# Buffers of a fused transformer kernel placed in another order, and the low parts of its routing stage issued later

## What is computed

```python
def reference(...):
    x = first_block(...)    # attention + MLP(4096), then pooling mixer + MLP(4096), final norm
    return second_block(x, ...)

def second_block(x, mem, ...):
    h = x
    # ssd branch, latent attention, merged through w_o, cross attention to mem (256 rows)
    h = h + hierarchical_moe(rms_norm_2(h, norm_moe), w_rg, b_rg, w_re, b_re, w_gate, w_up, w_down)
    return rms_norm_2(h, norm_final)

def hierarchical_moe(h, ...):   # 4 groups x 8 experts = 32, width 256, two per token
    g_sel = argmax(t @ w_rg + b_rg)                 # group
    top_v, top_i = top_k(e_logits[g_sel], 2)        # two experts in it
    act = silu(t @ w_gate[e]) * (t @ w_up[e]) * combine[:, e]
    y = sum_e act @ w_down[e]
```

## Time and profile before

| | us |
|---|---|
| median of three runs | 1258.95 |
| the profiled execution | 1256.77 |
| its span (first to last instruction) | 1254.9 |
| mean granted clock of TensorE | 0.992 |

### The profile page before, as it was taken

One profiled execution on the slowest core, in us unless ns is written; L12 is line 12 of the kernel. 1 busy time (PEld: TensorE's weight loads), 2 busy tenths in 40 slices (PEclk: granted clock), 3 DMA queues, 4 the chain that ended last, 5 costly groups with the idle time before them and its releaser, 6 DMA issues. The chain is left out here.

```text
span 1254.9 us, 22421 instructions
## 1 busy us (share of the span) xinstructions
PE 1205.3 (96%) x9064; PEld 1025.1 (82%) x9064; DVE 783.8 (62%) x1316; ACT 608.1 (48%) x992; POOL 99.1 (8%) x102
## 2 busy tenths in 40 slices
PE   9999999999999999999999999999999999999982
PEld 7989999999999999899999988999999833333320
DVE  6876655556755555999899889869645552222113
ACT  6665544454544454767655586665454321111101
POOL 0000100000100000000000030010100004431301
PEclk9999999999999999999999999999999999999997
DMA  9653655554455565455544384355544989999993
GB/s 305 192 182 122 202 172 195 174 196 135 156 181 182 186 200 161 134 168 168 164 140 135 87 258 167 103 202 168 172 165 130 413 326 404 411 404 406 405 406 139
DMA packets 161045, 270.28 MB, mean 215 GB/s; under 512 B 17625, under 2 KB 126142, under 8 KB 156862
## 3 DMA queue, kind: packets, MB, share of 16 engines
q1 hardware_dynamic: 149872, 260.53, 59.9%
q0 software_dynamic: 10720, 8.42, 2.4%
q10 hardware_dynamic: 366, 0.12, 0.0%
HBM read 287.89 MB, written 13.63 MB: 240 GB/s over the span
## 5 line engine op out<-in xcount | busy, mean ns | idle before, releaser
L2118 DVE TENSOR_TENSOR weights_parts<-ring,weights_parts 128x1024 fp32r<-128x1024 f32 (+3 forms) x312 | 363.5, 1186 | 149.2 <-ACT weights_parts L1541 148.8
L1541 ACT ACTIVATE weights_parts<-ring 128x1024 fp32r<-128x1024 f32 (+3 forms) x312 | 308.6, 1009 | 157.2 <-PE psum L885 156.6
L883 PE MATMUL psum<-xnorm_parts,weights_parts 128*128 128x256 f32 x852 | 245.4, 288 | 4.9 <-DVE xnorm_parts L2266 2.0
L884 PE MATMUL psum<-xnorm_parts,weights_parts 128*128 128x256 f32 x852 | 239.4, 281 | 0.0
L885 PE MATMUL psum<-xnorm_parts,weights_parts 128*128 128x256 f32 x852 | 239.2, 281 | 0.0
L883 PE MATMUL psum<-expert_cols,weights_parts 128*128 128x256 f32 (+1 forms) x688 | 194.7, 283 | 3.2 <-DVE expert_cols L2136 2.0
L885 PE MATMUL psum<-expert_cols,weights_parts 128*128 128x256 f32 (+1 forms) x688 | 192.0, 279 | 0.0
L884 PE MATMUL psum<-expert_cols,weights_parts 128*128 128x256 f32 (+1 forms) x688 | 192.0, 279 | 0.0
L883 PE MATMUL psum<-hidden_parts,weights_parts 128*128 128x256 f32 x640 | 181.9, 284 | 2.7 <-DVE hidden_parts L2589 1.7
L884 PE MATMUL psum<-hidden_parts,weights_parts 128*128 128x256 f32 x640 | 180.5, 282 | 0.0
L885 PE MATMUL psum<-hidden_parts,weights_parts 128*128 128x256 f32 x640 | 180.4, 282 | 0.0
(11 more groups left out here) (449 smaller groups left out, 1725.8 us busy)
## 6 DMA issues: line engine op xcount, KB each, us to landing
ring<-in_mlp_w_up SPq DMA_DIRECT2D x32, 1024.0 KB, 5.5
ring<-in_mlp_w_down SPq DMA_DIRECT2D x32, 1024.0 KB, 4.9
ring<-in_w_in SPq DMA_DIRECT2D x30, 1024.0 KB, 5.4
ring<-in_attn_w_qkv SPq DMA_DIRECT2D x12, 1024.0 KB, 6.8
expert_raw<-in_w_exp_gate SPq DMA_DIRECT2D x22, 512.0 KB, 11.4
expert_raw<-in_w_exp_up SPq DMA_DIRECT2D x22, 512.0 KB, 12.5
ring<-in_w_exp_down SPq DMA_DIRECT2D x9, 1024.0 KB, 16.8
expert_raw<-in_w_exp_down SPq DMA_DIRECT2D x9, 1024.0 KB, 16.4
```

The lines of the kernel that those rows point to most:

```text
L883: pe.matmul(out, lh, rh, start=start, stop=False, **more)
L884: pe.matmul(out, lh, rl, start=False, stop=False, **more)
L1541: ins = act.activation(high, src, ACT.Copy)
L2118: ins = dve.tensor_tensor(low, src, high.bitcast(F32), ALU.subtract)
```

## The change

The buffers are asked for in another order: consts, router_b and dskip first, then ring, weights_parts, xnorm_parts, hidden_parts, the other buffers whose size is a multiple of 512 bytes, the arena, and the small ones last. Names, sizes and the arena's inner layout stay.

In the routing stage VectorE's first low part goes from between the masks and the rank to behind both sort matrices; one unused operation (a comparison into `mask`) is left out. TensorE takes all high parts it can before the low ones, and drops the 8 fillers after the sort. The first expert step's windows are copied in two pieces: k 0 to 3 as soon as the first four evictions are done, k 4 to 7 at the end.

```diff
+        consts = sb("consts_sb", [P, C_N])
+        router_b = sb("router_b", [P, EG + NE])
+        dskip = sb("dskip", [P, ZT])
         ring = sb("ring", [P, SLOTS, SLOT])
-        consts = sb("consts_sb", [P, C_N])
         with nc.sbuf_tensor("expert_weights", [P, 2 * UNITS * UNIT], F32) as w_plain:
             pass
         w_parts = sb("weights_parts", [P, 2 * UNITS * UNIT], F32R)
-        cols = sb("cols", [P, 2 * P])
-        dskip = sb("dskip", [P, ZT])
-        dskip_all = sb("dskip_all", [P, SH])
-        ssd_par = sb("ssd_par", [SH, 4])
...
         results = sb("results", [P, M_END - M_COLS])
         arena_rest = sb("arena_rest", [P, ARENA - M_END])
+        dskip_all = sb("dskip_all", [P, SH])
+        ssd_par = sb("ssd_par", [SH, 4])
...
             warm(16)
-            pe.wait_ge(s["nat_low"], 1)
+            pe.wait_ge(s["nat_high"], TB)
             pe.wait_ge(s["sort_ready"], TB)
             for k in range(4):
                 sorted_part(k, 0, 0, True, False)
-                sorted_part(k, 0, 1, False, False)
-            pe.wait_ge(s["nat_high"], TB)
             pe.wait_ge(s["sort_ready"], 2 * TB)
             for k in range(4):
                 sorted_part(k, 1, 0, False, False)
-            pe.wait_ge(s["nat_low"], TB)
-            for k in range(4):
-                sorted_part(k, 1, 1, False, True).then_inc(s["sorted_full"], 1)
             for k in range(4, KT):
+                sorted_part(k, 0, 0, True, False)
+            for tb in range(TB):
+                pe.wait_ge(s["nat_low"], tb + 1)
+                for k in range(4):
+                    mm = sorted_part(k, tb, 1, False, tb == TB - 1)
+                    if tb == TB - 1:
+                        mm.then_inc(s["sorted_full"], 1)
+            for k in range(4, KT):
+                sorted_part(k, 1, 0, False, False)
                 for tb in range(TB):
-                    for half in range(2):
-                        mm = sorted_part(k, tb, half, tb == 0 and half == 0, tb == TB - 1 and half == 1)
+                    mm = sorted_part(k, tb, 1, False, tb == TB - 1)
                 mm.then_inc(s["sorted_full"], 1)
-            pe.wait_ge(s["sorted_even"], 2)
-            pe.wait_ge(s["sorted_odd"], 2)
-            warm(8)
...
-                if part == 0:
+                if n == 0 and part == 0:
+                    pe.wait_ge(s["sorted_even"], 3)
+                    pe.wait_ge(s["early_first"], 1)
+                    pe.wait_ge(s["early_second"], 1)
+                elif n == 0 or part == 0:
                     pe.wait_ge(s["window_first"], n + 1)
                     pe.wait_ge(s["window_second"], n + 1)
...
+                    act.wait_ge(s["sorted_even"], 2)
+                    act.wait_ge(s["sorted_odd"], 2)
+                    act.activation(xe[:, 0, 0, 0:4], cols_by_place[:, 0:4, bass.ds(columns[0], ROWS)],
+                                   ACT.Copy).then_inc(s["early_first"], 1)
...
-            for n in range(2):
-                window_first(n, columns[n])
+            act.activation(xe[:, 0, 0, 4:], cols_by_place[:, 4:, bass.ds(columns[0], ROWS)],
+                           ACT.Copy).then_inc(s["window_first"], 1)
+            window_first(1, columns[1])
...
-            nat_low(0)
             b = wait_full("rank", 0)
...
-            dve.tensor_scalar(rt("mask"), rank, ROWS - 0.5, None, ALU.is_gt)
...
+            nat_low(0)
             nat_low(1)
...
+                    dve.wait_ge(s["sorted_odd"], 2)
+                    dve.wait_ge(s["sorted_even"], 2)
+                    dve.tensor_copy(xe[:, 0, 1, 0:4], cols_by_place[:, 0:4, bass.ds(columns[0], ROWS)]).then_inc(
+                        s["early_second"], 1)
```

More of the change, by code:

```diff
@@ L383, in build_two_blocks @@
         hid_parts = sb("hidden_parts", [P, 4 * 512], F32R)
+        x = sb("xres", [P, KT, TOK])
         sq = sb("squares", [P, KT, TOK])
+        sin_t = sb("sin_t", [P, TOK])
+        cos_t = sb("cos_t", [P, TOK])
         cb_sb = sb("cb_sb", [P, TOK])
         std = sb("std", [P, 3, TOK])
-        std_col = sb("std_col", [P, 2, TB])
-        gain_both = sb("gain_both", [P, KT])
-        smax = sb("smax", [P, 3, 2])
-        ssum = sb("ssum", [P, 3, 2])
-        srec = sb("srec", [P, 3, 2])
+        cols = sb("cols", [P, 2 * P])
         rope_a = sb("rope_a", [P, 2, TOK])
@@ L396, in build_two_blocks @@
         acum_parts = sb("acum_parts", [2 * SH, TOK], F32R)
-        unit_pair = sb("unit_pair", [2 * SH, SH], F32R)
-        dtn = sb("dtn", [P, 5, SH])
-        router_w = sb("router_w", [P, KT, EG + NE])
-        router_b = sb("router_b", [P, EG + NE])
         zeros = sb("zeros", [P, 512], BF16)
-        eps_col = sb("eps_col", [P, 3])
-        place_ids = sb("place_ids", [P, 4], I32)
-        slot_rows = sb("slot_rows", [P, NB], I32)
-        window_ids = sb("window_ids", [1, SLOTS_ALL], I32)
-        more_rows = sb("more_rows", [P, 2 * MORE], I32)
-        half_rows = sb("half_rows", [P, 2, 2 * MORE], I32)
         with nc.sbuf_tensor("arena", [P, ARENA], F32) as arena:
@@ L414, in build_two_blocks @@
         arena_rest = sb("arena_rest", [P, ARENA - M_END])
+        dskip_all = sb("dskip_all", [P, SH])
+        ssd_par = sb("ssd_par", [SH, 4])
+        std_col = sb("std_col", [P, 2, TB])
+        gain_both = sb("gain_both", [P, KT])
+        smax = sb("smax", [P, 3, 2])
+        ssum = sb("ssum", [P, 3, 2])
+        srec = sb("srec", [P, 3, 2])
+        unit_pair = sb("unit_pair", [2 * SH, SH], F32R)
+        dtn = sb("dtn", [P, 5, SH])
+        router_w = sb("router_w", [P, KT, EG + NE])
+        eps_col = sb("eps_col", [P, 3])
+        place_ids = sb("place_ids", [P, 4], I32)
+        slot_rows = sb("slot_rows", [P, NB], I32)
+        window_ids = sb("window_ids", [1, SLOTS_ALL], I32)
+        more_rows = sb("more_rows", [P, 2 * MORE], I32)
+        half_rows = sb("half_rows", [P, 2, 2 * MORE], I32)
         psum = ctx.enter_context(nc.psum_tensor("psum", [P, 8, 512], F32))
@@ L545, in build_two_blocks @@
             "rstd_ready", "masks_ready", "cleared", "nat_high", "nat_low", "sort_ready", "sorted_full", "sorted_even",
-            "sorted_odd", "windows_ready", "window_first", "window_second", "ids_ready", "places_ready", "more_ready",
+            "sorted_odd", "windows_ready", "window_first", "window_second", "early_first", "early_second", "ids_ready", "places_ready", "more_ready",
             "silu_done", "act_done", "act_full", "act_copied", "y_first", "y_second", "final_sums", "final_root",
@@ L1451, in _ @@
                 sorted_part(k, 1, 0, False, False)
-            pe.wait_ge(s["nat_low"], TB)
-            for k in range(4):
-                sorted_part(k, 1, 1, False, True).then_inc(s["sorted_full"], 1)
             for k in range(4, KT):
+                sorted_part(k, 0, 0, True, False)
[7 more added lines that the diff above has]
+                sorted_part(k, 1, 0, False, False)
                 for tb in range(TB):
-                    for half in range(2):
-                        mm = sorted_part(k, tb, half, tb == 0 and half == 0, tb == TB - 1 and half == 1)
+                    mm = sorted_part(k, tb, 1, False, tb == TB - 1)
                 mm.then_inc(s["sorted_full"], 1)
-            pe.wait_ge(s["sorted_even"], 2)
-            pe.wait_ge(s["sorted_odd"], 2)
-            warm(8)
             def gate_up(n, part):
                 buf = n % 2
-                if part == 0:
+                if n == 0 and part == 0:
[3 more added lines that the diff above has]
+                elif n == 0 or part == 0:
                     pe.wait_ge(s["window_first"], n + 1)
                     pe.wait_ge(s["window_second"], n + 1)
+                if part == 0:
                     if n >= 2:
@@ L2841, in _ @@
             dve.wait_ge(s["sorted_even"], KT // 2)
-            for n in range(2):
-                window_second(n, columns[n])
+            dve.tensor_copy(xe[:, 0, 1, 4:], cols_by_place[:, 4:, bass.ds(columns[0], ROWS)]).then_inc(s["window_second"], 1)
+            window_second(1, columns[1])
             def by_halves(t):
```

3 lines of the change are left out of this document (removed).

## The result

The kernel after takes 1261.96 us (median of seven runs, 1261.63 to 1265.06), the kernel before 1259.22 in the runs beside it: ratio 1.0032, interval 1.0022 to 1.0042. It is slower by 0.3% (by the two medians alone 0.2%), where 1255.2, 0.3% faster, had been forecast. The profiled execution took 1262.1 (span 1260.3), 5.3 more than that of before.

What follows compares the result with a forecast made beforehand. TensorE's matmul count times their distance was taken as the bound up to the expert stage, where DMA queues count too. 1256.8 - 1.8 (buffer order) - 2.0 (routing) = 1253.0, plus 2.2 for the median: 1255.2 us; range 1221 to 1264.

Steps and rivals of the forecast that it cites:

- The bound: Up to the expert stage, time is the number of TensorE matmuls times their start-to-start distance; TensorE busy 96% of the span.
- Part 1: New buffer order: 4476 three-part products go from 118.1 to 117.7 ns, 1.8 us less; no instruction added or removed.
- The forecast's own sign of being wrong: Three-part products: the forecast is wrong if their pace changes by more than 1 ns either way.
- The other bound: Three-part products: everything at the fast pace of 113.5 ns, 31 us less.
- The floor of 112.5: TensorE: weight loads beside one-column matmuls come 112.5 ns apart, taken as the floor; products reaching it give 38 us less.
- Part 2: Routing stage: low parts later, fillers dropped, early window copies; experts begin 2.0 us sooner, bounds 1.0 to 2.6.
- DMA destinations: Loads into the moved buffers: aligned destinations costed at 0, as the aligned buffer's landing time lay between the others.
- Rival D: Expert stage: loads gain from aligned destinations, 1.6%, 3 us on the full stretch, time 1252; chance 0.04.
- C: Three-part products: both streams at the same residue modulo 512 run slower, 1.4 ns each, 10 us more, 1267; chance 0.18.
- A: Three-part products: with both operands at 0 nearly all lock at 113.5 ns, time 1226; chance 0.28.
- B: Three-part products: buffer order gives nothing, the 0.4 ns belong to the streams, not the place; time 1257.0; chance 0.15.
- E: Routing stage: early copies wait for both engines' evictions, end after the sort; gain 1.0, time 1256.2; chance 0.35 with forecast.

Runs made afterwards that it cites:

- The probe: Kernel of nothing but runs of 48 float32r products on zeros, each run with other start bytes for both operands; 113.3 to 120.0 ns a matmul with 256 columns.

## Why the prediction was wrong

- **The bound.** Right: the end of the dense stages moved with the pace, by 11.5 us for 12.8 in the products.
- **Part 1, the pace.** Wrong, and this is the step that failed: "pairs with equal residue have two paces here, and I have seen the fast one rarely in this form; pairs with unequal residue have not shown it", residues taken modulo 64. The probe shows that the residue modulo 64 sorts nothing: distances 0, 64, 128 and 192 give 120.0, 117.8, 118.7 and 113.3. The period is 256 bytes, and no other distance is slower than 0 (with the stationary operand at 16 the probe gave 120.0 too). The data of before didn't contain distance 0, and I put the new case into a class with the two I had seen. The forecast's own sign of being wrong, a pace that changes by more than 1 ns, is there: 2.0. By the table the change costs 4572 x 1.7 (distance 224) + 2064 x 2.3 (64) + 288 x 3.3 (32) + 192 x 5.4 (192, a mixture) = 14.5 us; the means of the traces give 7116 x 1.96 = 13.9, and 11.5 arrived at the last product.
- **The bounds of part 1.** The loss was bounded by 1.4 ns from two placements; it was 2.0 in the mean. The other bound was sound, and other places do reach it nearly: 114.05 against 113.5. The floor of 112.5, read from loads beside one-column matmuls, isn't quite one: the probe's runs with 192 and 224 columns go at 111.6.
- **Part 2.** Right: 2.3 us against 2.0 (bounds 1.0 to 2.6). The part of it ahead of the sort was 0.6 instead of 0.3 (3.27 us from first filler to first sort matmul instead of 3.88), behind the sort 1.7 as forecast. The low parts stayed hidden: the sort took 8.1 us.
- **DMA destinations.** Costed at 0, worth 3.8 (3.4 with the destinations alone). I compared destinations within one run, where all loads share 16 full engines. With the other destinations aligned, the loads into the two buffers that stayed land sooner too (17.7 to 16.6, 16.6 to 16.0 us), so such a comparison can't show the effect; what tells is the rate of the stretch. By the Trainium skill, "DMA: Bandwidth & Descriptors", section "How a descriptor splits into AXI transactions", a descriptor that doesn't start on a multiple of 256 bytes also fetches the bytes between the boundary below and its start. For 4096 bytes at 96 past a boundary I work out 131 beats of 32 bytes instead of 128, an estimate of some 2%. The page speaks of what is read, and here it is the side written to that moved; the size agrees with the runs, 407 against 415 GB/s. Rival D, beside which this stood, had a chance of 0.04, since rows 6 spoke against it.
- **The rivals.** C happened, in its place (both streams at the same residue) and its direction, at 13.9 us instead of 10; it was joined by D. Its chance was 0.18. That the time lies inside the stated range is luck: without the 3.8 us of the expert stage, costed at 0, it would be 1265.8, past the 1264. A was right in that 113.3 is to be had, wrong in where. B fell: the 0.4 ns did belong to the place. E fell.
- **The sum.** 1256.8 + 11.5 - 2.3 - 3.8 = 1262.2 against 1262.1 profiled. All its terms are differences between these two traces, so they must add up; what bears them out are the kernels with one part each: 12.7 and -4.2 us with the order alone, 2.3 less with the routing alone, 3.4 less in the expert stage with the destinations alone.
- The Trainium skill, "TensorE: Matmul & The Clock Gate", section "Step-by-step: what each phase is for", says that loading the next weights takes nothing from the running matmul. For 224 columns no run contradicts it. For 256 the pace goes from 113.3 to 120.0 ns by the place of one operand against the other, which that sentence doesn't provide for. That the two reads take from each other is the nearest reading, since pairs shifted together keep their pace; no run shows it more directly.

## What to carry to other kernels

With products like these (float32r, 256 columns behind 128x128 weights that change every time), the place of both operands is a parameter of the kernel: measure the pace from start to start in unbroken runs, make a table of it by a kernel of some 50 short runs, and don't put both operands on the same residue modulo 256. Aligning everything moves two things at once, so price the destinations of full-rate DMA and the operands of matmuls apart. A class seen in the data (two paces for "matched" pairs) says nothing of a value that the data don't hold.

## What the runs showed of the hardware

- float32r products with 256 columns behind 128x128 weights go at 113.3 to 120.9 ns by the places of the operands, at a granted clock of 1.00; with 192 or 224 columns they go at 111.6 at all four places tried. With both parts of an operand at one place, the slowest is both operands at the same residue modulo 256 (120.0 ns, 288 cycles at 2.4 GHz; 113.3 are 272).
- At distances 64 and 192 there are two steady paces, 113.3 and 117.8 ns. At 192 the moment of entry chose in the probe (four and four of eight), and in the kernels whole stretches of over 100 us keep one pace from run to run. Two kernels at distance 192 spread by 9 and 11 us between executions. That the entry is the reason is not shown: one trace of each is kept, 3 us of the 9 can be the clock, and the kernel with one small buffer moved, at the same distance for most of its products, spread by 1.1.
- With the high part of the weights at 64, the low part at 192 and both moving parts at 0 modulo 256, the fast pace was taken from all eight entries. With the low moving part at 128 besides, it was the slowest pattern.
- Destinations on multiples of 512 bytes instead of 96 and 128 past one gave 2% more in a stretch that is full of 4 and 8 KB rows, 415 against 407 GB/s. With expert_raw and results at 256 it was 415 too.
